# Attention scores, transpositions and products in units of 512 queries instead of 256

## The chip, the cores and the metric

The kernel runs on one core of one Trainium2 chip. The metric is the device time of one execution in microseconds (us), the median over the runs. PE is the matrix engine, DVE the vector engine, ACT the scalar engine, POOL the GpSimd engine, SP the engine that issues most loads.

## The reference

A decoder trunk of two layers on x (1024 positions, 1024 features, float32). Layer 0 is a gated linear recurrence, layer 1 is attention with a forget gate; each is followed by a SwiGLU layer, and a final norm ends it. The change touches only the attention:

```
q = (xn @ w_q) in 16 heads of 64; k, v, c come once from the residual stream
for each block of 128 queries q0:q1:
    s = q[q0:q1] @ k[:q1].T * scale + c[q0:q1, None] - c[None, :q1]
    s = where(mask, s, -inf)            # causal
    p = softmax(s)
    out[q0:q1] = p @ v[:q1]
```

## The kernel before

Every float32 product is made of three products of float32r parts (a high and a low part of each operand, `wh`/`wl`, `xh`/`xl`). Outside the attention the kernel is a stream of 128x512 matmuls. The attention runs over 8 **pairs** of heads (function `pair` of each engine, i = 0 to 7; pairs 1 to 6 are alike and are called steady here, the first and last pair have lists of their own). All engines walk through one list of steps, `pair_steps`, and each does its share of each step, in that order; semaphores tie them.

A pair has 2 heads, and a head's 1024 queries are cut into **ranges** of 256; one range of one head is a **unit**, so a pair has 8 units, in the order of `RANGE_ORDER` [3, 0, 2, 1]. The steps are:
- `A`, `B`: the value projection of this pair, 24 matmuls 128x512 each (one half of the positions), drained by DVE; `X`: eight PE transpositions of the values, copied by ACT (`X`) and DVE (`Y`).
- `S0`, `S1` in unit u: scores of the next unit's query blocks (128 queries each, width up to the diagonal) on PE; DVE subtracts the mask and takes the row maximum (L3121), ACT the exponential with the row sum (L2169). Score tiles alternate between PSUM slots 0 and 1, and a score waits until the exponential of the tile two before it has freed its slot.
- `T0`, `T1`, ...: transpositions of the probabilities (128x128 on PE, L1479) of two key blocks into `t_ps`; ACT copies them to `pth` (high part, L2204), DVE subtracts to `ptl` (low part, L3128). Both are double buffered. The first `T` of a unit waits for all exponentials of the unit.
- `V0`, `V1`, ...: products of values with `pth` and `ptl` (L1492), 256 or 128 columns wide, accumulated in `o_ps`.
- `O`: ACT copies the low half of the result (`o_low`, L2209), DVE adds it (L3137). The next unit's `V0` waits for it.
- `p`: three matmuls 128x512 of the next pair's K and Q projections, 32 `p` a pair, strewn between the others as cover (in the last pair 28 `p` of the output projection). `R`: one transposition of the row sums.

Between two pairs ACT and DVE split the next K and Q in high and low parts (L2126 to L2142 and L3047, L3053), and weight pieces are split by ACT (L1625, `HI_AT`) and DVE (L2276, `LO_AT`). POOL multiplies weights by gains (L928), scales a finished pair's output (L943) and writes the selector rows (L933).

Of the kernel before, what the change touches and what calls it, by code (L numbers as in the profile page):

```python
# [4 lines left out]
F32 = mybir.dt.float32  # L5
# [6 lines left out]
P = 128  # L12
# [37 lines left out]
class FeedForward:  # L50
# [8 lines left out]
    def first_part(self, n, half):  # L59
# [10 lines left out]
RANGE_ORDER = [3, 0, 2, 1]  # L70
UNIT_STEPS = [
# [8 lines left out]
]  # L80
FIRST_UNIT = "p p p X Y p T0 T1 p T2 V0 V1 T3 S0 S1 V2 V3"
LAST_UNIT_STEPS = [
# [8 lines left out]
]  # L91
PAIR_START = "A S0 S1 B"
FIRST_START = "A B S0 S1"
# [19 lines left out]
def pair_steps(with_p, first):  # L113

    steps = [(-1, s) for s in (FIRST_START if first else PAIR_START).split()]
    units = UNIT_STEPS if with_p else LAST_UNIT_STEPS
    for u, unit in enumerate([FIRST_UNIT] + units[1:] if first else units):
        steps += [(u, s) for s in unit.split()]
    steps.append((len(UNIT_STEPS), "O"))
    return steps  # L120


def hawk_fox_yoco(nc, x, norm_mix, norm_ffn, w_ffn_in, w_ffn_out, w_rec_in, conv_w, conv_b,
# [21 lines left out]
    RANGES = QB // 2  # L145
# [25 lines left out]
    tiles.plan("att", [1, 0, 1] + [0, 1] * (UNITS - 1) + [0], PAIRS).plan("attE", [1, 2, 0, 1, 2, 0, 1, 2, 2])  # L171
# [13 lines left out]
    T_PAIR = RANGES * (RANGES + 1)  # L185
    OUT_HI_AT = {(-1, "A"): 0, (0, "Y"): 1, (UNITS - 2, "T2"): 2}
    OUT_LO_AT = {(-1, "S1"): 0, (1, "S1"): 1, (UNITS - 2, "V2"): 2}
# [9 lines left out]
    with ExitStack() as life:  # L197
# [85 lines left out]
        with ExitStack() as att:  # L283
# [17 lines left out]
            probs = [sb(f"probs{b}", [P, 2, S // (b + 1)], F32, att) for b in range(2)]  # L301
# [4 lines left out]
            o_low = [sb(f"o_low{b}", [HD, 2 * P], F32, att) for b in range(2)]  # L306
# [48 lines left out]
        o_ps = ps[3][:, 0:2 * P]  # L355
# [369 lines left out]
        def s_tile(i, u, half):  # L725
            return tiles.use("att", half if u == 0 else 2 * u + half + 1, i)
# [6 lines left out]
        def vt_tile(i):  # L733
            return tiles.use("att", 2, i)

        def rsum_tile(i):
            return tiles.use("att", 2 * UNITS + 1, i)
# [9 lines left out]
        def tiles_before(u):  # L747

            return sum(range_of(v) + 1 for v in range(u))

        def pt_used_at(i, t):

            u = max(v for v in range(UNITS) if tiles_before(v) <= t)
            if t - tiles_before(u) == range_of(u):
                return o_filled, i * UNITS + (u + 1)
            return pt_used, i * (T_PAIR - UNITS) + (t + 1 - u)

# [148 lines left out]
        def _(pool):  # L906
# [131 lines left out]
        def _(pe):  # L1038
# [410 lines left out]
            def scores(i, u, half):  # L1449

                j, n = u // RANGES, 2 * range_of(u) + half
                acc = claim(s_tile(i, u, half))
                w = (n + 1) * P
# [9 lines left out]
            def blocks_of(r, m):  # L1463

                if m < r:
                    return [(2 * m, 0, 0), (2 * m + 1, 0, 2 * P)]
                return [(2 * m, 0, 0), (2 * m + 1, 1, 2 * P)]

            def transposes(i, u, m):
                t = tiles_before(u) + m  # L1470
                if m == 0:
                    for half in range(2):
                        slot, n = s_tile(i, u, half)
                        pe.wait_ge(drained[slot], n)
                if t >= 2 or not (isinstance(i, int) and i == 0):
                    pe.wait_ge(ptl_ready, i * T_PAIR + (t - 1))
                for kb, q0, col in blocks_of(range_of(u), m):
                    for q in range(q0, 2):
                        last = pe.transpose(t_ps[t % 2][:, col + (q - q0) * P:col + (q - q0 + 1) * P],  # L1479
                                            probs[u % 2][:, q, kb * P:(kb + 1) * P], ident[:, :])  # L1480
                last.then_inc(t_filled, 1)

            def values(i, u, m):
# [10 lines left out]
                last.then_inc(o_filled if m == r else pt_used, 1)  # L1494
# [8 lines left out]
            def pair(i, uses, with_p=True):  # L1503
# [3 lines left out]
                for u, step in pair_steps(with_p, is_first(i)):  # L1507
                    m = int(step[1]) if len(step) > 1 else 0
                    if step in "AB":
                        half = "AB".index(step)  # L1510
# [4 lines left out]
                        elif is_first(i):  # L1515
                            pe.wait_ge(f_drained, 2)
                        for k in range(KT):
                            projection_part(f_bank(step), uses["V"], half, k, v_filled)
                        f += 1
                        f_read = f_before(i) + f  # L1520
# [92 lines left out]
        def _(act):  # L1613
# [501 lines left out]
            act.activation(ps[3][0:HEADS, :], probs[0][0:HEADS, 0, :], ACT.Ln).then_inc(forget_act, 1)  # L2115
# [44 lines left out]
            def exponentials(i, u, half):  # L2160
                n, w = 2 * u + half, (2 * range_of(u) + half + 1) * P
                slot, _ = s_tile(i, u, half)
                col = u // RANGES * QB + 2 * range_of(u) + half
# [5 lines left out]
                act.activation(probs[u % 2][:, half, 0:w], ps[slot][:, score_cols(w)], ACT.Exp,  # L2169
# [11 lines left out]
            def pair(i, uses, with_p=True):  # L2181
# [4 lines left out]
                for u, step in pair_steps(with_p, is_first(i)):  # L2186
# [23 lines left out]
                    if with_p and (u, step) in HI_AT:  # L2210
                        kind = HI_AT[u, step]
# [57 lines left out]
        def _(dve):  # L2269
# [735 lines left out]
            z, e = probs[1][0:HEADS].rearrange("p a n -> p (a n)"), rinv[0:HEADS, :]  # L3005
            one_e, over = probs[0][0:HEADS, 0, :], probs[0][0:HEADS, 1, :]
# [88 lines left out]
            def pair(i, uses, with_p=True):  # L3095
# [4 lines left out]
                for u, step in pair_steps(with_p, is_first(i)):  # L3100
                    m = int(step[1]) if len(step) > 1 else 0
                    if step in "AB":
                        half = "AB".index(step)
# [3 lines left out]
                        dve.tensor_tensor(kv_tmp[:, h], f_bank(step), rstd[:, h], ALU.mult).then_inc(f_drained, 1)  # L3107
# [7 lines left out]
                    elif step[0] == "S":  # L3115
                        n, wide = 2 * (u + 1) + m, (2 * range_of(u + 1) + m + 1) * P
# [139 lines left out]
```

## Time and profile before

| | us |
|---|---|
| median of 3 runs (2226.34 to 2226.66) | 2226.61 |
| the profiled execution, its own time | 2225.23 |
| its span from first to last instruction | 2223.4 |
| PE busy | 2198.2 |
| DVE busy | 1674.6 |
| ACT busy | 1181.7 |
| one steady pair (six of them) | 60.55 |

A busy PE means that some matmul is in flight. Matmuls are pipelined, so the distance between two starts, not the duration of one, is what a matmul takes of PE's time.

### The profile page before, as it was taken

To read this page: it belongs to the slowest core of one execution; us is meant where nothing else is said; L and a number is where in the kernel's file an instruction comes from. 1 tells how busy PE (TensorE), PEld (TensorE's weight loads), DVE (VectorE), ACT (ScalarE), POOL (GpSimd) and SP (SyncE) were. 2 spreads that over 40 slices of the span, in tenths; PEclk is the share of its full clock that TensorE was granted. 3 is DMA by queue.
4 is the path that set the end of the run, shared out by engine and by line. 5 is a ranking of instruction groups with operands and counts; after the bars stand their busy time and mean duration, and the time that the engine had idled before them with its cause. 6 is when DMAs were issued, how large, how long until landed. Compare 5 with 4: busy or idle time off the path is not lost.

```text
span 2223.4 us, 28679 instructions
## 1 busy us (share of the span) xinstructions
PE 2198.2 (99%) x10393; PEld 1831.4 (82%) x10393; DVE 1674.6 (75%) x2353; ACT 1181.7 (53%) x1873; POOL 361.2 (16%) x352
## 2 busy tenths in 40 slices
PE   8999999999999999999999999999999999999998
PEld 6888887888888888887888888888888888888886
DVE  7667788787778777688666766775777778888866
ACT  5543576355555555356666666754535555555525
POOL 4000000022222222021111111102002222222200
PEclk9999999999999999999999999999999999999999
DMA  5110300366676666431111111132136666666652
GB/s 152 48 60 26 95 15 24 133 133 133 133 133 133 131 125 124 134 115 29 39 30 39 39 39 39 30 105 76 38 133 120 127 121 127 128 127 130 129 167 86
DMA packets 208984, 208.03 MB, mean 94 GB/s; under 512 B 9705, under 2 KB 153297, under 8 KB 208849
## 3 DMA queue, kind: packets, MB, share of 16 engines
q0 software_dynamic: 39168, 75.51, 20.7%
q1 hardware_dynamic: 167952, 126.43, 19.1%
q10 hardware_dynamic: 1728, 4.31, 0.7%
q8 instruction: 81, 1.33, 0.2%
q14 instruction: 55, 0.44, 0.1%
HBM read 122.28 MB, written 83.95 MB: 93 GB/s over the span
## 4 chain that ended last, share of the span: by engine, by line
PE 93%; DVE 4%; issue 1%; ACT 1%; DMA 0%; ACTq 0%; DVEq 0%
PE ps L1244 37%; PE ps L1049 18%; PE ps L1332 14%; PE ps L1445 10%; PE ps L1492 3%; PE ps L1583 3%; PE ps L1479 3%; PE ps L1460 1%; PE ps L1459 1%; PE ps L1562 1%; PE ps L1134 0%; PE ps L1525 0%; PE ps L1098 0%; PE ps L1417 0%; PE ps L1400 0%
## 5 line engine op out<-in xcount | busy, mean ns | idle before, releaser
L977 POOL DMA_DIRECT2D spill<-c x256 | 223.7, 926 | 725.5 <-DVE c L2705 493.2
L2574 DVE TENSOR_TENSOR ring_l<-raw_ffn,ring_h 128x512 fp32r<-128x512 f32 x320 | 222.8, 699 | 154.5 <-ACT ring_h L1811 153.1
L1811 ACT ACTIVATE ring_h<-raw_ffn 128x512 fp32r<-128x512 f32 x320 | 199.0, 626 | 196.5 <-PE ps L1244 103.7
L1904 ACT ACTIVATE c<-ps 128x512 f32<-128x512 f32 x256 | 150.2, 597 | 13.2
L1445 PE MATMUL ps<-xh,wh_att 128*128 128x512 f32 x368 | 148.6, 404 | 1.6 <-DVE wl_att L2276 1.6
L1811 ACT ACTIVATE ring_h<-w_sum 128x512 fp32r<-128x512 f32 x112 | 69.5, 625 | 147.2 <-PE ps L1049 38.9
L2169 ACT ACTIVATE probs<-ps,nmax 128x896 f32<-128x896 f32 (+7 forms) x128 | 95.0, 742 | 99.2 <-DVE nmax L3121 97.3
L1445 PE MATMUL ps<-xh,wl_att 128*128 128x512 f32 x368 | 143.9, 391 | 0.0
L1445 PE MATMUL ps<-xl,wh_att 128*128 128x512 f32 x368 | 143.9, 391 | 0.0
L3128 DVE TENSOR_TENSOR ptl<-ps,pth 128x512 fp32r<-128x512 f32 (+1 forms) x160 | 96.9, 634 | 52.4 <-ACT pth L2204 51.0
L2705 DVE TENSOR_TENSOR c<-ps,c 128x512 f32<-128x512 f32 x192 | 123.5, 685 | 4.8 <-PE ps L1332 4.3
L2313 DVE TENSOR_TENSOR resid<-ps,resid 128x1024 f32<-128x1024 f32 x76 | 92.4, 1221 | 39.2 <-PE ps L1049 31.4
L2204 ACT ACTIVATE pth<-ps 128x512 fp32r<-128x512 f32 (+1 forms) x160 | 82.7, 553 | 34.2 <-PE ps L1479 24.3
L1332 PE MATMUL ps<-hl,ring_h 128*128 128x512 f32 x256 | 99.8, 390 | 0.0
L1332 PE MATMUL ps<-hh,ring_h 128*128 128x512 f32 x256 | 99.7, 390 | 0.0
L1332 PE MATMUL ps<-hh,ring_l 128*128 128x512 f32 x256 | 99.6, 389 | 0.0
L3121 DVE CUSTOM_DVE_ANT_0 ps<-ps,causal 128x896 f32<-128x896 f32 (+7 forms) x128 | 94.6, 774 | 0.0
L2574 DVE TENSOR_TENSOR ring_l<-w_sum,ring_h 128x512 fp32r<-128x512 f32 x112 | 76.7, 686 | 21.9 <-ACT ring_h L1811 21.9
L1479 PE MATMUL ps<-ident,probs 128*128 128x128 f32 x576 | 81.5, 275 | 2.8 <-DVE ptl L3128 1.2
L1445 PEld LDWEIGHTS ps<-xh,wl_att 128*128 128x128 f32 x368 | 69.1, 188 | 15.6
L1492 PE MATMUL ps<-pth,vs 128*128 128x256 f32 x320 | 80.6, 279 | 0.7 <-DVE ptl L3128 0.4
L1049 PE MATMUL ps<-rxh,wh 128*128 128x512 f32 x256 | 79.9, 393 | 0.2 <-issue 0.2
(411 smaller groups left out, 6295.4 us busy)
## 6 DMA issues: line engine op xcount, KB each, us to landing
spill<-c POOLq DMA_DIRECT2D x256, 256.0 KB, 6.0
raw_ffn<-in_w_ffn_in SPq DMA_DIRECT2D x88, 512.0 KB, 5.3
raw_ffn<-in_w_ffn_out SPq DMA_DIRECT2D x44, 512.0 KB, 7.2
resid<-spill SPq DMA_DIRECT2D x24, 512.0 KB, 6.9
raw<-in_w_rec_in SPq DMA_DIRECT2D x16, 512.0 KB, 5.6
spill<-resid POOLq DMA_DIRECT2D x16, 512.0 KB, 2.9
raw_att<-in_w_kvf SPq DMA_DIRECT2D x16, 512.0 KB, 4.1
xin<-in_x SPq DMA_DIRECT2D x4, 1024.0 KB, 9.8
```

The lines of the kernel that those rows point to most:

```text
L977: pool.dma_start(spill[m, :, half * BANK:(half + 1) * BANK], block[:, :], accum_op=ALU.add).then_inc(sem, 16)
L1049: last = pe.matmul(acc[:, h], w, v[:, h], start=(first and p == 0), stop=(final and p == 2))
L1244: last = pe.matmul(acc, w, v, start=(start and k == 0 and p == 0), stop=(k == 3 and p == 2), skip_group_check=True)
L1332: last = pe.matmul(acc, a, v, start=(i in (P1, P2, P5) and p == 0), stop=(p == 2), skip_group_check=True)
L1445: last = pe.matmul(acc, w, v[:, k, h], start=(k == 0 and p == 0), stop=(k == KT - 1 and p == 2))
L1479: last = pe.transpose(t_ps[t % 2][:, col + (q - q0) * P:col + (q - q0 + 1) * P], probs[u % 2][:, q, kb * P:(kb + 1) * P], ident[:, :])
L1492: last = pe.matmul(o_ps[:, q0 * P:2 * P], v, pt[t % 2][:, col:col + n], start=(kb == 0 and pt is pth), stop=(kb == 2 * r + 1 and pt is ptl))
L1811: act.activation(F.ring_h[slot][:, :], src, ACT.Copy).then_inc(F.unit_hi, 1)
L1904: act.activation(dst[:, :], y if what == "s5" else w, ACT.Copy).then_inc(out_tapped, 1)
L2574: dve.tensor_tensor(F.ring_l[slot][:, :], src, F.ring_h[slot][:, :].bitcast(F32), ALU.subtract).then_inc(F.unit_lo, 1)
L2705: dve.tensor_tensor(c, w if what == "C22" else y, c, ALU.add).then_inc(out_joined, 1)
L3128: dve.tensor_tensor(ptl[t % 2][:, 0:width], t_ps[t % 2][:, 0:width], pth[t % 2][:, 0:width].bitcast(F32), ALU.subtract).then_inc(ptl_ready, 1)
```

## The change

A unit is now one head and 512 queries: a pair has 4 units, with `RANGE_ORDER` [1, 0] (the upper 512 queries first). A unit has four score steps `S0` to `S3`, and 3 or 7 transposed tiles of up to 512 columns. The 36 transpositions of a head stay 36, and the ten tiles of a head that ACT and DVE copy stay ten (512 wide but the last of a unit, 256, where four were 384). The product of a key block with the probabilities is up to 512 columns wide. `o_low` and its addition are 512 wide and come 4 times a pair instead of 8. `B` is cut in two (`B`, `C`, 12 matmuls each) with `S2 S3` between them, and all step lists and the tables of when weights are split are written anew; POOL scales the weights of Q ahead of the last pair's output.

```
-RANGE_ORDER = [3, 0, 2, 1]
+RANGE_ORDER = [1, 0]
 UNIT_STEPS = [
-    "T0 T1 X p p Y S0 T2 T3 p V0 V1 S1 p p V2 V3",
...
+    "T0 T1 X p S0 Y p p T2 T3 V0 S1 V1 S2 p p V2 V3 T4 T5 S3 p p p T6 V4 V5 p V6",
+    "O T0 T1 S0 S1 p V0 p T2 p S2 p S3 p V1 V2 p",
+    "S0 p O T0 T1 S1 p p V0 T2 S2 p T3 p V1 T4 V2 S3 p p V3 T5 V4 T6 p p V5 V6",
+    "T0 p O T1 p T2 p V0 V1 p R p V2 p p p",
 ]
-FIRST_UNIT = "p p p X Y p T0 T1 p T2 V0 V1 T3 S0 S1 V2 V3"
+FIRST_UNIT_STEPS = [
+    "X p Y T0 T1 p S0 p V0 T2 T3 p V1 V2 T4 S1 S2 T5 V3 V4 p T6 S3 p p V5 V6",
...
 LAST_UNIT_STEPS = [
-    "T0 T1 X Y S0 T2 p T3 V0 V1 p S1 V2 V3",
...
+    "T0 X Y T1 T2 p p V0 T3 V1 S0 V2 T4 T5 V3 S1 p p V4 T6 p S2 S3 V5 V6",
...
-PAIR_START = "A S0 S1 B"
-FIRST_START = "A B S0 S1"
+PAIR_START = "A S0 S1 B S2 S3 C"
+FIRST_START = "A B C S0 S1 p p p S2 S3 p p"
+LAST_START = "A S0 S1 B S2 S3 C"
...
             def blocks_of(r, m):
-                if m < r:
-                    return [(2 * m, 0, 0), (2 * m + 1, 0, 2 * P)]
-                return [(2 * m, 0, 0), (2 * m + 1, 1, 2 * P)]
+                if m <= 4 * r:
+                    return [(m, 0, 0)]
+                if m == 4 * r + 1:
+                    return [(m, 1, 0), (m + 2, 3, 3 * P)]
+                return [(m, 2, 0)]
...
-                    n = (2 - q0) * P
+                    n = (4 - q0) * P
                     for pt in (pth, ptl):
-                        last = pe.matmul(o_ps[:, q0 * P:2 * P], v, pt[t % 2][:, col:col + n],
-                                         start=(kb == 0 and pt is pth), stop=(kb == 2 * r + 1 and pt is ptl))
...
+                        last = pe.matmul(o_ps[:, q0 * P:BANK], v, pt[t % 2][:, col:col + n],
+                                         start=(kb == 0 and pt is pth), stop=(kb == 4 * r + 2 and pt is ptl))
...
             def pool_pair(i, uses, next_k=None):
                 pool.wait_ge(ql_ready, i * 2 + 2)
-                pool.wait_ge(o_added, i * UNITS + 1)
+                gain_piece(uses["Q"], GAIN["Q"])
                 if not (isinstance(i, int) and i == 0):
                     scale_o(i - 1)
-                gain_piece(uses["Q"], GAIN["Q"])
-                pool.wait_ge(o_added, i * UNITS + 4)
+                pool.wait_ge(o_added, i * UNITS + 2)
```

The first place is PE in a steady pair, the products of values (`vs`) with `pth` and `ptl` at the end of the pair's first unit. Before, the last two tiles (`V2`, `V3`):

```order
L1492 MATMUL ps<-pth,vs 128x256
L1492 MATMUL ps<-ptl,vs 128x256
L1492 MATMUL ps<-pth,vs 128x256
L1492 MATMUL ps<-ptl,vs 128x256
L1492 MATMUL ps<-pth,vs 128x256
L1492 MATMUL ps<-ptl,vs 128x256
L1492 MATMUL ps<-pth,vs 128x128
L1492 MATMUL ps<-ptl,vs 128x128
L1479 MATMUL ps<-ident,probs 128x128 x3
```

Now, the same place (`T6 V4 V5 p V6`):

```order
L1495 MATMUL ps<-ident,probs 128x128 x2
L1508 MATMUL ps<-pth,vs 128x512
L1508 MATMUL ps<-ptl,vs 128x512
L1508 MATMUL ps<-pth,vs 128x384
L1508 MATMUL ps<-ptl,vs 128x384
L1508 MATMUL ps<-pth,vs 128x128
L1508 MATMUL ps<-ptl,vs 128x128
L1460 MATMUL ps<-xh,wh_att 128x512
L1460 MATMUL ps<-xl,wh_att 128x512
L1460 MATMUL ps<-xh,wl_att 128x512
L1508 MATMUL ps<-pth,vs 128x256
L1508 MATMUL ps<-ptl,vs 128x256
```

Fewer and wider matmuls carry the same columns: of the 64 of 256 columns and 16 of 128 in a pair, 24 of 512, 8 of 384, 8 of 256 and 8 of 128 remain in their place.

The second place is DVE at the start of a steady pair, from the splitting of the second head's K and Q to the first low parts of probabilities (`ISA` is the mask and maximum). Before:

```order
L3047 TENSOR_TENSOR kl<-kv_tmp,kh 64x1024
L3053 TENSOR_TENSOR qs<-q_tmp,qs 64x1024
L3107 TENSOR_TENSOR kv_tmp<-ps,rstd 128x512
L3121 ISA ps,nmax<-ps,causal 128x896
L3121 ISA nmax 128x1
L3121 ISA ps,nmax<-ps,causal 128x1024
L3121 ISA nmax 128x1
L2276 TENSOR_TENSOR wl_att<-raw_att,wh_att 128x1024
L3107 TENSOR_TENSOR kv_tmp<-ps,rstd 128x512
L3128 TENSOR_TENSOR ptl<-ps,pth 128x512 x2
```

Now:

```order
L3125 TENSOR_TENSOR kv_tmp<-ps,rstd 128x512
L3139 ISA ps,nmax<-ps,causal 128x640
L3139 ISA nmax 128x1
L3139 ISA ps,nmax<-ps,causal 128x768
L3139 ISA nmax 128x1
L2294 TENSOR_TENSOR wl_att<-raw_att,wh_att 128x1024
L3139 ISA ps,nmax<-ps,causal 128x896
L3139 ISA nmax 128x1
L3139 ISA ps,nmax<-ps,causal 128x1024
L3139 ISA nmax 128x1
L3125 TENSOR_TENSOR kv_tmp<-ps,rstd 128x512
L3146 TENSOR_TENSOR ptl<-ps,pth 128x512 x2
```

Four score tiles, not two, now stand ahead of the first transposition, and the two widest come last, behind the weight split.

## Rows read from the trace of the kernel before

**Rows 1.** The page, busy time, share of the span and instructions.
```profile
PE 2198.2 (99%) x10393; PEld 1831.4 (82%) x10393; DVE 1674.6 (75%) x2353; ACT 1181.7 (53%) x1873; POOL 361.2 (16%) x352
```

**Rows 2.** Busy time by window (start:end, length), granted clock, DMA share, GB/s.
```profile
1010.00:1072.00 62.00, 58.25 (x341) 49.75 (x340) 45.99 (x80) 42.53 (x78) 7.77 (x5) 1.00 0.10 27
...
1138.55:1199.10 60.55, 60.35 (x355) 52.49 (x354) 41.40 (x77) 38.51 (x74) 10.12 (x6) 1.00 0.13 35
...
1430.00:1492.80 62.80, 61.36 (x356) 52.06 (x356) 51.47 (x87) 44.70 (x82) 0.00 (x0) 1.00 0.31 100
```

**Rows 3.** PE in order of time (start, us), one steady pair.
```profile
1142.03 1.03 PE L1479 MATMUL ps<-ident,probs 128*128 128x128 f32 x8
1143.13 1.06 PE L1525 MATMUL ps<-ident,kv_tmp 128*128 128x128 f32 x8
...
1144.27 0.39 PE L1445 MATMUL ps<-xl,wh_att 128*128 128x512 f32 x1
...
1145.60 0.95 PE L1479 MATMUL ps<-ident,probs 128*128 128x128 f32 x7
...
1146.62 0.40 PE L1445 MATMUL ps<-xl,wh_att 128*128 128x512 f32 x1
...
1148.27 0.40 PE L1445 MATMUL ps<-xh,wh_att 128*128 128x512 f32 x1
...
1149.66 0.28 PE L1492 MATMUL ps<-pth,vs 128*128 128x256 f32 x1
...
1150.37 0.22 PE L1492 MATMUL ps<-pth,vs 128*128 128x128 f32 x1
...
1150.69 0.52 PE L1479 MATMUL ps<-ident,probs 128*128 128x128 f32 x3
...
1153.26 0.22 PE L1492 MATMUL ps<-pth,vs 128*128 128x128 f32 x1
...
1153.71 0.39 PE L1445 MATMUL ps<-xl,wh_att 128*128 128x512 f32 x1
...
1154.64 0.40 PE L1445 MATMUL ps<-xh,wl_att 128*128 128x512 f32 x1
1155.17 1.07 PE L1479 MATMUL ps<-ident,probs 128*128 128x128 f32 x8
```

**Rows 4.** DVE in order of time, the same pair and the next one's start.
```profile
1152.25 0.82 DVE L3121 CUSTOM_DVE_ANT_0 ps<-ps,causal 128x640 f32<-128x640 f32 x1
...
1152.99 1.00 DVE L3121 CUSTOM_DVE_ANT_0 ps<-ps,causal 128x768 f32<-128x768 f32 x1
...
1197.05 0.69 DVE L3107 TENSOR_TENSOR kv_tmp<-ps,rstd 128x512 f32<-128x512 f32 x1
1197.66 1.09 DVE L3121 CUSTOM_DVE_ANT_0 ps<-ps,causal 128x896 f32<-128x896 f32 x1
...
1198.66 1.26 DVE L3121 CUSTOM_DVE_ANT_0 ps<-ps,causal 128x1024 f32<-128x1024 f32 x1
```

**Rows 5.** PE in order of time, first score matmul of the next pair.
```profile
1195.41 0.39 PE L1459 MATMUL ps<-kl,q 128*128 128x512 f32 x1
```

**Rows 6.** ACT in order of time, an exponential and its read of the sum.
```profile
1200.02 1.12 ACT L2169 ACTIVATE probs<-ps,nmax 128x1024 f32<-128x1024 f32 x1
1201.03 0.19 ACT L2169 ACTIVATION_READ_ACCUMULATOR probs<-ps,nmax 128x1 f32 x1
```

**Rows 7.** PE in order of time, the first pair's two longest waits.
```profile
1018.81 0.47 PE L1445 MATMUL ps<-xh,wh_att 128*128 128x512 f32 x1 [1.63 <-DVE wl_att L2276]
...
1025.11 0.66 PE L1479 MATMUL ps<-ident,probs 128*128 128x128 f32 x4 [0.83 <-DVE ptl L3128]
```

**Rows 8.** POOL in order of time.
```profile
1001.82 1.95 POOL L1022 MEMSET kl<- 64x1024 f32 x2
...
1151.93 2.40 POOL L943 TENSOR_TENSOR resid<-resid,rinv 128x1024 f32 x1 [28.94 <-DVE resid L3137]
```

**Rows 9.** Line 2276 on DVE: duration in ns, shortest, median, longest.
```profile
L2276 DVE TENSOR_TENSOR wl_att<-raw_att,wh_att x31: 1215/1220/1946, 973.4 to 1541.0; 128x1024 fp32r<-128x1024 f32 x31
```

More of the change, by code:

```diff
@@ L113, in pair_steps @@
 def pair_steps(with_p, first):
-    steps = [(-1, s) for s in (FIRST_START if first else PAIR_START).split()]
-    units = UNIT_STEPS if with_p else LAST_UNIT_STEPS
-    for u, unit in enumerate([FIRST_UNIT] + units[1:] if first else units):
+    start, units = (FIRST_START, FIRST_UNIT_STEPS) if first else (PAIR_START, UNIT_STEPS)
+    if not with_p:
+        start, units = LAST_START, LAST_UNIT_STEPS
+    steps = [(-1, s) for s in start.split()]
+    for u, unit in enumerate(units):
         steps += [(u, s) for s in unit.split()]
@@ L144, in hawk_fox_yoco @@
     QB = S // P
-    RANGES = QB // 2
+    RANGES = QB // 4
     UNITS = 2 * RANGES
@@ L184, in hawk_fox_yoco @@
     SUMMED = {seg: n * RUN_SUMS for seg, n in STAT.items()}
-    T_PAIR = RANGES * (RANGES + 1)
-    OUT_HI_AT = {(-1, "A"): 0, (0, "Y"): 1, (UNITS - 2, "T2"): 2}
-    OUT_LO_AT = {(-1, "S1"): 0, (1, "S1"): 1, (UNITS - 2, "V2"): 2}
+    T_PAIR = 2 * sum(4 * r + 3 for r in range(RANGES))
+    OUT_HI_AT = {(-1, "S1"): 0, (0, "T1"): 1, (3, "T1"): 2}
+    OUT_LO_AT = {(-1, "C"): 0, (0, "S1"): 1, (3, "V0"): 2}
     O_SPLITS = PAIRS
@@ L300, in hawk_fox_yoco @@
             vs = sb("vs", [P, 2, QB, 2, HD], F32R, att)
-            probs = [sb(f"probs{b}", [P, 2, S // (b + 1)], F32, att) for b in range(2)]
+            probs = [sb(f"probs{b}", [P, n], F32, att) for b, n in enumerate((26 * P, 10 * P))]
             pth = [sb(f"pth{b}", [P, BANK], F32R, att) for b in range(2)]
@@ L305, in hawk_fox_yoco @@
             rinv = sb("rinv", [P, S], F32, att)
-            o_low = [sb(f"o_low{b}", [HD, 2 * P], F32, att) for b in range(2)]
+            o_low = [sb(f"o_low{b}", [HD, BANK], F32, att) for b in range(2)]
             nmax = sb("nmax", [P, 2 * QB], F32, att)
@@ L723, in range_of, with s_tile, vt_tile, rsum_tile @@
             return RANGE_ORDER[u % RANGES]
-        def s_tile(i, u, half):
-            return tiles.use("att", half if u == 0 else 2 * u + half + 1, i)
+        def s_tile(i, u, n):
+            return tiles.use("att", n if u == 0 else 4 * u + n + 1, i)
+        def vt_tile(i):
+            return tiles.use("att", 4, i)
+        def rsum_tile(i):
+            return tiles.use("att", 4 * UNITS + 1, i)
+        def wide_of(u, n):
+            return (4 * range_of(u) + n + 1) * P
         def score_cols(w):
@@ L731, in score_cols, with probs_of @@
             return slice(first, first + w)
[L733 to L737, printed above, removed]
+        def probs_of(u, n):
+            first = sum(wide_of(u, q) for q in range(n))
+            return probs[u % 2][:, first:first + wide_of(u, n)]
         def f_before(i):
@@ L747, in tiles_before, with tile_wide @@
         def tiles_before(u):
-            return sum(range_of(v) + 1 for v in range(u))
+            return sum(4 * range_of(v) + 3 for v in range(u))
+        def tile_wide(u, m):
+            return BANK if m < 4 * range_of(u) + 2 else 2 * P
         def pt_used_at(i, t):
             u = max(v for v in range(UNITS) if tiles_before(v) <= t)
-            if t - tiles_before(u) == range_of(u):
+            if t - tiles_before(u) == 4 * range_of(u) + 2:
                 return o_filled, i * UNITS + (u + 1)
@@ L1447, in projection_part, with scores @@
                     last.then_inc(filled, 1)
[L1449 to L1453, printed above, removed]
+            def scores(i, u, q):
+                j, n, w = u // RANGES, 4 * range_of(u) + q, wide_of(u, q)
+                acc = claim(s_tile(i, u, q))
                 at = score_cols(w)
@@ L1471, in transposes @@
                 if m == 0:
-                    for half in range(2):
-                        slot, n = s_tile(i, u, half)
-                        pe.wait_ge(drained[slot], n)
+                    for n in range(2, 4):
+                        slot, count = s_tile(i, u, n)
+                        pe.wait_ge(drained[slot], count)
                 if t >= 2 or not (isinstance(i, int) and i == 0):
@@ L1514, in pair @@
                                 pe.wait_ge(forget_dve, INVERSE_USED)
-                        elif is_first(i):
+                        elif step == "A" and is_first(i):
                             pe.wait_ge(f_drained, 2)
[L1517 to L1520, printed above, removed]
+                        for k in {"A": range(KT), "B": range(KT // 2), "C": range(KT // 2, KT)}[step]:
+                            projection_part(f_bank("AB"[half]), uses["V"], half, k, v_filled)
+                        if step != "B":
+                            f += 1
+                            f_read = f_before(i) + f
                     elif step == "X":
```

75 lines of the change are left out of this document (40 added, 35 removed), and 20 rows, old and new, of tables (FIRST_UNIT_STEPS, LAST_UNIT_STEPS, UNIT_STEPS).

## The prediction

> **What bounds the kernel now.** I read the page first: PE is busy for 2198.2 us of the span, 99% [rows 1], so time can only come from PE's own work or from its few waits. The change touches the attention alone, some 480 us. The windows give each stretch of it: a steady pair takes 60.55 us, PE is busy 60.35 of them at the full clock (1.00, the upper of its two levels) while DVE is busy 41.40 and ACT 38.51 [rows 2]. The first pair's window has 62.00 - 58.25 = 3.75 us of idle PE, the last one's 62.80 - 61.36 = 1.44 us [rows 2]. So DVE and ACT do not bound by volume; they bound only where their chain from PE back to PE is longer than the work put between. Then PE's list in order of time, read by the distance of starts [rows 3]:
> - From 1148.27 to 1149.66 stand six 512-wide matmuls: 0.232 us each. From 1149.66 to 1150.37 six 256-wide ones: 0.118 each. Twice 0.118 is 0.237, hardly more than one 512.
> - A high/low couple of 128 columns is dear: 1153.26 to 1153.71 holds the couple and one 512, so the couple takes 0.45 - 0.23 = 0.22 us, against 0.236 for twice its columns.
> - Seven transpositions and one 512 take 1.02 (1145.60 to 1146.62), eight and one 1.14 (1143.13 to 1144.27): about 0.11 each, and some 0.03 for each change from a run of them to something else.
> - Waits of a steady pair: 1142.03 to 1143.13 is 1.10 for eight transpositions worth 0.87 (0.23, the second half of V isn't drained), 1154.64 to 1155.17 is 0.53 for one 512 (0.30, the exponentials are late), 1150.37 to 1150.69 is 0.32 for a couple of 0.22 (0.10). Together 0.63 us a pair.
>
> **PE's work after.** Columns, transpositions, scores and projections stay the same in number. In a pair 48 matmuls of 256 become 24 of 512: 48 x 0.118 = 5.66 against 24 x 0.232 = 5.57, a gain of 0.10. The other 16 of 256 and 8 couples of 128 (1.89 + 1.76 = 3.65) become 8 of 384, 8 of 256 and 4 couples of 128. No product of 384 is in the rows; by the line through 256 and 512 it is 0.175. That makes 1.40 + 0.94 + 0.88 = 3.22, a gain of 0.43. I count the runs of transpositions in the lists: 13 in a steady pair before, 16 now, 3 x 0.03 = 0.1 lost. Net 0.43 us a pair; over 8 pairs **3.5 us**. Its bounds: 0.12 us a pair if a narrow couple costs its columns alone (then only the 0.10 and 0.02 more stay), and 0.65 if the wide ones run at the best distance and the run changes cost nothing: 1.0 to 5.2 us. I take 3.5, since most of it rests on the directly read 0.22.
>
> The Trainium skill ("TensorE: Matmul & The Clock Gate", section "Back-to-back issue gap") gives the distance of warm matmuls as columns by 2.4 GHz plus 2.5 ns. By it a matmul less is worth 2.5 ns, and the 32 fewer of a pair 0.08 us, an estimate from that page of 0.6 us in all; the trace's 0.232 and the dear 128 couple disagree with it here, and the measurement decides.
>
> **The new waits of a steady pair.** The rewritten lists decide these, so I laid out by hand each place where PE comes back to DVE or ACT.
>
> *Pair start.* Today's first score begins at 1195.41 [rows 5], while DVE drains A from 1197.05 and starts its first reduction at 1197.66 [rows 4]: DVE is late by its four K and Q splits, and nothing in the change takes those away. New on PE from 1195.41: S0 0.57 (640 columns in two passes, by the distances above), S1 0.68, B 12 x 0.23, S2 0.80, ending at 1200.2, S3 until 1201.2, C until 1203.9. New on DVE from 1197.66: 0.74 and 0.91 for the two (distances in [rows 4]: 1152.25 to 1152.99, the second from its 1.00), 1.22 for the weight split [rows 9], free at 1200.5; then 1.0 for 896 columns and 1.26 + 0.1 for 1024 [rows 4], done at 1202.9. ACT's exponential and sum take 1.2 [rows 6]: 1204.1. The first transposition, due at 1203.9, waits 0.2 us. C is drained in DVE's free time right after, so the old 0.23 ahead of the values' transpositions goes. ACT also splits Q's weights here (about 1.1, with the transposed tile queued behind it); two runs of work, the eight transpositions of values and three `p` (0.7 each), cover that before V0.
>
> *Third unit.* S3 of the second unit is followed by p V1 V2 p S0 p, about 0.7 + 0.5 + 0.2 + 0.7 + 0.1 + 0.7 = 2.9 us, ahead of T0. Its reduction and exponential take 1.3 + 1.2, with DVE about 0.5 late from the tile and the reduction of S2: 3.0. Wait 0.1. V0 of the third unit comes 2 `p` after T1 and needs `o_low`, two tiles on ACT, and the low part on DVE: 2.0 to 2.2 against 1.6 plus the score: 0.1 at most.
>
> *The rest.* Every other V stands at least 1.4 us (two `p`) or another T and V behind its T. `O` is needed only at the next V0; POOL's moved work feeds splits that are due tens of us later; loads wait for the same splits and land long ahead. I price these at nothing; if the cover of one is short by half a `p`, it costs 0.3 us a pair.
>
> So 0.4 us, and I say 0.5 for what restarts cost that no layout shows, stays of 0.63: **0.8 us** gained over six pairs. Bounds: from all waits gone (-3.8) to 0.5 more than now in each pair (+3).
>
> **First and last pair.** In the first, 1.63 us went for the weight split of K and 0.83 for the low part ahead of T2 [rows 7]. The first stays (DVE's chain to it is the same, and PE comes 0.5 us earlier by narrower scores, whose other half is done later). In the new list T2 stands two `p` and more behind T0, so 0.83 goes, but V0 then waits for about 0.5 (exponential of S3, the copies of values, the low part). I take **0.6** less, bounds -2 to +1. The last pair has the same chains with DVE fuller (51.47 busy of 62.80 [rows 2]): I take no change, bounds -1 to +1.5.
>
> **Sum**, against the profiled execution: span 2223.4 - 3.5 - 0.8 - 0.6 = 2218.5. Around the span lie 2225.23 - 2223.4 = 1.8 us; the median lies 1.4 above that execution's own time. So 2226.6 - 4.9 = **2221.7 us**. From now on no difference means within 0.2%, 4.45 us: below 2222.16 is faster.
>
> **Rivals.**
> 1. *The waits eat it.* PE keeps the 0.43 us a pair, but hand layouts miss a wait of 0.5 a pair somewhere in 28 new V and T places. For it: the new pair start has no spare, and the lists were laid for one copy of each chain. Against: DVE and ACT have some 20 us a pair free. Time: 2226.6 - 3.5 + 8 x 0.5 = 2227, with half of that wait 2225.
> 2. *The narrow couple is not dear*, or the wide product brings a cost of its own (0.118 to 0.232 is already just double). Work gain 0.12 a pair, waits as forecast: 2226.6 - 1.0 - 1.4 = 2224.2.
> 3. *POOL holds DVE up: slower.* POOL's gain of Q and its scaling (2.40 us [rows 8]) now start when Q is split, on top of DVE's reductions and weight split at the pair start, where PE waits. One row speaks for it: a DVE weight split took 1946 ns instead of 1220 [rows 9] while POOL filled `kl` at 1001.82 [rows 8]. If every DVE instruction there grew by 0.6 of itself, 4 us would grow by 2.4, and T0 would wait 2.4 more in 7 pairs: +17 - 5 = 2238. It decides from 0.7 + 0.6 a pair on. Against: POOL's scaling at 1151.93 to 1154.33 ran over two reductions, which took 0.82 and 1.00 us as always [rows 4, 8].
> 4. *More than forecast*: all three steady waits gone and 0.65 of work: 2226.6 - 5.2 - 3.8 - 0.6 = 2217.
>
> The Trainium skill ("SBUF — State Buffer", section "Terms") says that DVE and GpSimd share a port pair that one of them locks for a whole instruction while the other is fully blocked. By that the scaling's 2.40 us would be paid whole in seven pairs, 17 us, an estimate of the same size as this rival's; the two reductions that ran over POOL's scaling don't show it.
>
> **How the numbers follow.** Forecast 0.48 (its own range 2219.5 to 2224), rival 1 0.23, rival 2 0.12, rival 3 0.06, rival 4 0.11. Of the forecast's cases some two thirds lie below 2222.16, of rival 4's all, of rival 1's and 2's one in five: faster 0.50. Slower is rival 3 and a tail of rival 1 over 2231: 0.08. Same 0.42. The range runs from rival 4 to the milder half of rival 1: 2216.5 to 2227.
>
> **What would show it.** Right: steady pairs of about 60.0 us; 512-wide products 0.23 apart, 384-wide 0.175; a wait of 0.2 to 0.4 at the pair's first transposition and none at the values'; PE idle of the first pair down to about 3. Wrong: a steady pair at 60.4 or more; waits named "DVE ptl" or "ACT probs" of over 0.3 us in the third unit; DVE reductions longer than 0.82 and 1.00 at the pair start while POOL is busy.

## The result, and the profile after

The changed kernel takes 2234.68 us (median of 6 runs, 2233.60 to 2235.92), the kernel before 2226.30 beside it (6 runs, 2225.53 to 2226.66). The ratio is 1.004, 95% interval 1.003 to 1.005: slower by 0.4%, where 2221.7 was forecast. The profiled execution took 2235.92 us, with a span of 2234.1.

The page of the kernel after, busy time (compare [rows 1]):

```profile
PE 2197.1 (98%) x10137; PEld 1817.7 (81%) x10137; DVE 1683.5 (75%) x2321; ACT 1177.1 (53%) x1841; POOL 360.0 (16%) x352
```

PE has 256 matmuls fewer and 1.1 us less of busy time, and yet the span grew by 10.7 us. So PE stands idle more, or is slower. DVE, with 32 instructions fewer, is busy 8.9 us longer: the first hint. The windows of the kernel after, as in [rows 2] (start:end, length; busy time of PE, of its weight loads, of DVE, ACT and POOL; granted clock, DMA share, GB/s): first pair, a steady pair, last pair, and a short piece of the first and of the last.

```profile
1010.00:1074.00 64.00, 61.26 (x317) 50.22 (x316) 46.80 (x77) 43.57 (x75) 7.73 (x5) 0.97 0.11 32
1138.10:1199.50 61.40, 59.50 (x321) 49.99 (x320) 42.94 (x73) 37.97 (x70) 10.08 (x6) 1.00 0.13 35
1435.00:1505.00 70.00, 66.18 (x341) 54.52 (x341) 53.52 (x86) 45.25 (x79) 0.00 (x0) 0.98 0.30 91
1019.00:1023.00 4.00, 3.73 (x10) 2.95 (x11) 1.83 (x5) 1.88 (x4) 0.00 (x0) 0.57 0.49 131
1472.00:1477.00 5.00, 4.07 (x13) 3.25 (x14) 4.70 (x9) 1.25 (x3) 0.00 (x0) 0.66 0.15 60
```

The steady pair of this window takes 61.40 us (61.64 on average over pairs 1 to 6), not 60.0, with 1.90 us of idle PE, where it had 0.20. And the granted clock, 1.00 in all of [rows 2], falls to its lower level in two places of the attention. The three starts that part the attention, PE in order of time (first score of pair 1, first score of the last pair, start of the projection behind the attention):

```profile
1074.95 0.30 PE L1473 MATMUL ps<-kl,q 128*128 128x320 f32 x1
...
1444.81 0.30 PE L1473 MATMUL ps<-kl,q 128*128 128x320 f32 x1
...
1502.97 0.62 PE L1600 MATMUL ps<-xh,b21h 128*128 128x512 f32 x2
```

Before, these three stand at 1074.31, 1437.61 and 1492.60. The differences, with those of two experiments below (each against the kernel before, in us of the profiled spans):

| | after | experiment 1 (late scaling) | experiment 8 (all edits) |
|---|---|---|---|
| up to pair 1 (first pair) | +0.64 | +0.50 | -1.99 |
| pairs 1 to 6 | +6.56 | -3.64 | -3.62 |
| last pair | +3.17 | +3.14 | -0.07 |
| from there to the end | +0.33 | +0.40 | -0.62 |
| span | +10.7 | +0.4 | -6.3 |

The largest waits come from the view that groups PE's waits (engine, what waited, for whom: us in total, times, longest). The line left out is the wait for the program's first load, 6.4 us after and 6.6 before:

```profile
PE ps L1495 <- ACT probs L2186: 11.1, 7, 1.9
...
PE ps L1579 <- DVE resid L3174: 2.6, 1, 2.6
PE ps L1460 <- DVE wl_att L2294: 2.1, 1, 2.1
```

**The pair start.** PE's first transposition (L1495) waits for the exponentials in each pair; the six steady pairs' waits make up 10.9 of the 11.1 us. "ACT probs" is only the last link. The chain of waits of one pair start, by start, length and what:

```profile
1202.60 0.06 DVE nmax L3139
1202.66 3.08 DVE wl_att L2294
1205.73 1.01 DVE ps L3139
...
1206.80 0.94 DVE ps L3139
...
1209.03 0.20 ACT probs L2186
...
1209.47 1.07 PE ps L1495 x8
```

The weight split stands in it with 3.08 us. The durations in DVE's list for the same place, in order of time:

```profile
1200.25 0.69 DVE L3125 TENSOR_TENSOR kv_tmp<-ps,rstd 128x512 f32<-128x512 f32 x1
1200.86 0.82 DVE L3139 CUSTOM_DVE_ANT_0 ps<-ps,causal 128x640 f32<-128x640 f32 x1
...
1201.60 1.00 DVE L3139 CUSTOM_DVE_ANT_0 ps<-ps,causal 128x768 f32<-128x768 f32 x1
...
1202.52 3.21 DVE L2294 TENSOR_TENSOR wl_att<-raw_att,wh_att 128x1024 fp32r<-128x1024 f32 x1
1205.65 1.09 DVE L3139 CUSTOM_DVE_ANT_0 ps<-ps,causal 128x896 f32<-128x896 f32 x1
```

And POOL's:

```profile
1200.41 1.90 POOL L944 TENSOR_TENSOR raw_att<-raw_att,vec 128x1024 f32<-128x1024 f32 x1 [17.48 <-DVE qs L3071]
1202.26 2.38 POOL L959 TENSOR_TENSOR resid<-resid,rinv 128x1024 f32 x1
```

POOL's scaling starts 0.26 us ahead of the split and ends at 1204.64. The split ends at 1205.73, 1.09 later: it looks as if it had waited for the scaling and then run its usual time. The drain and the two reductions, which lie over POOL's gain, keep their 0.69, 0.82 and 1.00 us. What sets them apart is their operands: each of them reads one from PSUM (`ps`), the split reads both of its own (`raw_att`, `wh_att`) from SBUF.

**The last pair.** PE, SP and DVE in order of time:

```profile
1472.93 0.50 PE L1579 MATMUL ps<-xh,wh_att 128*128 128x512 f32 x1 [2.57 <-DVE resid L3174]
```

```profile
1468.90 0.82 SPq L896 DMA_DIRECT2D resid<-spill  x2
```

```profile
1467.65 1.22 DVE L3110 TENSOR_TENSOR xl<-resid,xh 128x1024 fp32r<-128x1024 f32 x1
1472.18 0.69 DVE L3174 TENSOR_TENSOR resid<-ps,resid 128x512 f32<-128x512 f32 x1 [3.31 <-DMA resid<-spill]
```

PE needs its PSUM bank drained (L3174), the drain adds a reloaded piece of the residual, and SP sends for that piece only when DVE has made the fifth low part of the output (L3110, step `V5` of the first unit), at 1468.87. That is 24.1 us behind the first score of the last pair; before, this load was issued at 1454.58, 17.0 us behind it. Behind the wait the clock is down: the matmuls of 512 columns that start from 1473.63 to 1476.19 stand 0.42 to 0.43 us apart, not 0.23 (granted 0.66 in the window above).

**The first pair.** PE waits 2.08 us where [rows 7] has 1.63, and the matmuls behind the wait stand 0.43 apart, not 0.23:

```profile
1019.27 0.68 PE L1460 MATMUL ps<-xh,wh_att 128*128 128x512 f32 x1 [2.08 <-DVE wl_att L2294]
1019.74 0.63 PE L1460 MATMUL ps<-xl,wh_att 128*128 128x512 f32 x1
1020.17 0.63 PE L1460 MATMUL ps<-xh,wl_att 128*128 128x512 f32 x1
```

### The profile page after: what moved, and what is told of

It is laid out like the page before. It is cut to its first block, busy times and chain, and to the rows that moved or that the text cites. A ratio compares the mean times of both kernels' runs of the same rounds, so it can differ in the third digit from the quotient of the medians.

```text
span 2234.1 us, 27984 instructions
## 1 busy us (share of the span) xinstructions
PE 2197.1 (98%) x10137; PEld 1817.7 (81%) x10137; DVE 1683.5 (75%) x2321; ACT 1177.1 (53%) x1841; POOL 360.0 (16%) x352
## 4 chain that ended last, share of the span: by engine, by line
PE 88%; DVE 7%; issue 2%; ACT 2%; DMA 1%; ACTq 0%; POOL 0%; DVEq 0%; POOLq 0%
PE ps L1259 37%; PE ps L1064 18%; PE ps L1347 14%; PE ps L1460 7%; PE ps L1508 3%; PE ps L1495 3%; PE ps L1600 3%; DVE wl_att L2294 1%; DVE ps L3139 1%; PE ps L1474 1%; PE ps L1473 1%; DVE kl L3065 1%; PE ps L1579 1%; DVE qs L3071 0%; PE ps L1149 0%
## 5 line engine op out<-in xcount | busy, mean ns | idle before, releaser
L2186 ACT ACTIVATE probs<-ps,nmax 128x640 f32<-128x640 f32 (+7 forms) x128 | 94.9, 742 | 125.4 <-DVE nmax L3139 124.3
L3139 DVE CUSTOM_DVE_ANT_0 ps<-ps,causal 128x640 f32<-128x640 f32 (+7 forms) x128 | 95.6, 768 | 14.7 <-PE ps L1474 14.4
L944 POOL TENSOR_TENSOR raw_att<-raw_att,vec 128x1024 f32<-128x1024 f32 x24 | 45.3, 1898 | 371.0 <-DVE resid L3155 211.2
L1495 PE MATMUL ps<-ident,probs 128*128 128x128 f32 x576 | 83.1, 273 | 11.5 <-ACT probs L2186 11.1
L1495 PEld LDWEIGHTS ps<-ident,probs 128*128 128x128 f32 x576 | 68.7, 141 | 28.4 <-DVE kv_tmp L3125 13.2
```

The costliest lines, as they stand in the source:

```text
L3139: dve.tensor_tensor_reduce(out=ps[slot][:, score_cols(wide)], in0=ps[slot][:, score_cols(wide)], in1=causal[:, S - wide:S], scale=-1.0, sc ...
```

## The experiments

All ratios are against the kernel before, run on the same chip.

**1. The scaling put late.** POOL waits for the addition of the new pair's first unit before it scales the finished pair's output; nothing else differs from the changed kernel.

```
                 gain_piece(uses["Q"], GAIN["Q"])
                 if not (isinstance(i, int) and i == 0):
+                    pool.wait_ge(o_added, i * UNITS + 1)
                     scale_o(i - 1)
```

> The changed kernel, only POOL's scaling of a finished pair's output moved behind the second unit's result (one wait). Theory A (POOL's scaling and DVE's weight split, both between SBUF tiles, exclude each other): the weight split at a steady pair's start falls from 3.2 us to 1.22, the wait ahead of the pair's first transposition from 1.8 to some 0.2 us, a steady pair from 61.4-61.6 us to 59.8, and the time from 2234.7 to about 2224. Theory B (the chain at the pair's start is too long by its own list: four K and Q splits, four reductions, one weight split): the split's length doesn't depend on POOL, the pair stays above 61 us and the time above 2232.

Measured: 2225.32 us (10 runs, 2223.84 to 2226.09), ratio 0.9997 (0.9987 to 1.0007): 9.4 us of the loss are back by this one wait. DVE of this kernel at a pair start, and its window of a steady pair:

```profile
1198.94 1.22 DVE L2295 TENSOR_TENSOR wl_att<-raw_att,wh_att 128x1024 fp32r<-128x1024 f32 x1
1200.29 1.10 DVE L3140 CUSTOM_DVE_ANT_0 ps<-ps,causal 128x896 f32<-128x896 f32 x1
```

```profile
1137.10:1196.84 59.74, 59.60 (x321) 50.03 (x321) 41.30 (x73) 38.10 (x69) 10.14 (x7) 1.00 0.12 36
```

The split is back at 1.22. The pair from one gain of POOL to the next takes 59.74 us, and pairs 1 to 6 together 359.66, 59.94 each. The first, last and end stretches stay as in the changed kernel (table above).

**2. POOL's new order alone, in the kernel before.** Units of 256 and all old lists, but POOL's gain of Q first and the scaling right behind it, without the first wait.

```
-                pool.wait_ge(o_added, i * UNITS + 1)
+                gain_piece(uses["Q"], GAIN["Q"])
                 if not (isinstance(i, int) and i == 0):
                     scale_o(i - 1)
-                gain_piece(uses["Q"], GAIN["Q"])
```

> The kernel before with only POOL's order of the changed one: the gain of Q first, the scaling right behind it, no wait for a result. Theory A: POOL's scaling then runs from about 1199.0 to 1201.4 on the old clock, over the weight split that began at 1199.84; the split takes about 2.8 us instead of 1.22, the drain of V's second half behind it and the values' transpositions are about 1.4 us later, and a steady pair goes from 60.55 to about 62; the time to about 2235. The two reductions ahead of it keep 0.82-1.26 us. Theory B: nothing over 0.2 us a pair changes, 2226 to 2228.

Measured: 2225.91 us (10 runs, 2225.30 to 2226.35), ratio 1.000 (0.9991 to 1.001). The hold-up is there, its price isn't: I had expected about 2235. POOL and DVE of this kernel at a pair start:

```profile
1138.89 2.41 POOL L943 TENSOR_TENSOR resid<-resid,rinv 128x1024 f32 x1
```

```profile
1138.45 1.27 DVE L3120 CUSTOM_DVE_ANT_0 ps<-ps,causal 128x1024 f32<-128x1024 f32 x1
...
1139.63 2.76 DVE L2275 TENSOR_TENSOR wl_att<-raw_att,wh_att 128x1024 fp32r<-128x1024 f32 x1
1142.63 0.69 DVE L3106 TENSOR_TENSOR kv_tmp<-ps,rstd 128x512 f32<-128x512 f32 x1 [0.25 <-PE ps L1444]
```

The split again ends 1.09 behind the scaling (1142.39 against 1141.30). But in the old list both reductions that the first transposition needs stand ahead of the split, and 24 matmuls of `B` (5.4 us) are under way. The next thing on DVE, the drain, has to wait for PE, not PE for it. So the early scaling costs only together with the new list, in which the two widest reductions stand behind the split.

**3. The split put behind the reductions.** The other way round: POOL stays as in the changed kernel, and DVE splits K's weights after the reductions of `S2` and `S3`. The scaling then lies over a reduction that reads PSUM.

```
-LO_AT = {(-1, "S1"): "K", (1, "S1"): "Q", (3, "V0"): "nextV"}
+LO_AT = {(-1, "S3"): "K", (1, "S1"): "Q", (3, "V0"): "nextV"}
```

> The changed kernel with one entry of LO_AT moved: in steady pairs VectorE splits K's weights behind the reductions of S2 and S3, not ahead of them. POOL is left as it is, so its scaling now lies over these two reductions, which read and write PSUM. Theory A (only a VectorE instruction whose operands all lie in SBUF is held up until POOL's instruction has ended): the two reductions keep their 1.09 and 1.26 us, the split, started at about the scaling's end, takes 1.2 to 1.5 us, the wait of 1.80 us at the first transposition falls to about 0.3, and the time is the one of the kernel with the late scaling, about 2225.5. Theory B (POOL's scaling holds up whatever VectorE runs then): the reductions grow by about 2 us together and the first transposition still waits 1.5 us or more; about 2234. Theory C (the split costs because it stands on the chain at all, 1.22 of its 3.21 us, and POOL's share is small): half of the gain, about 2230.

Measured: 2224.87 us (11 runs, 2223.49 to 2225.51), ratio 0.9994 (0.9985 to 1.0003). Theory A stands, B and C fall. POOL and DVE of this kernel:

```profile
1198.22 2.39 POOL L959 TENSOR_TENSOR resid<-resid,rinv 128x1024 f32 x1
```

```profile
1199.83 1.10 DVE L3139 CUSTOM_DVE_ANT_0 ps<-ps,causal 128x896 f32<-128x896 f32 x1 [1.21 <-PE ps L1474]
...
1200.93 1.23 DVE L3139 CUSTOM_DVE_ANT_0 ps<-ps,causal 128x1024 f32<-128x1024 f32 x1
...
1202.08 1.22 DVE L2294 TENSOR_TENSOR wl_att<-raw_att,wh_att 128x1024 fp32r<-128x1024 f32 x1
```

The reduction of 896 columns runs 0.78 us under the scaling (1199.83 to 1200.61) and takes its 1.10. It starts when PE has written its tile, not when POOL is done. Pairs 1 to 6 take 359.61 us, the same as in experiment 1. Two edits on two engines that share only this, that split and scaling no longer meet, give the same time.

**4. The first pair's split one drain earlier.**

```
-FIRST_LO_AT = {(-1, "C"): "K", (0, "S3"): "Q", (3, "T0"): "nextV"}
+FIRST_LO_AT = {(-1, "A"): "K", (0, "S3"): "Q", (3, "T0"): "nextV"}
```

> The changed kernel, in the first pair alone the low part of K's weights is made by DVE ahead of the drain of V's second half instead of behind it. Theory A (PE's gap of 2.24 us ahead of the first p lets the granted clock fall to its lower level, which costs more than the gap itself): the gap shrinks by 0.6 us to 1.6, the clock from 1019 to 1023 stays at 1.00 as in the kernel before, whose gap was 1.8, and the time falls by 0.6 + 1.6 = 2.2 us. Theory B (the low clock has another cause, such as its place in the program): only 0.6 us come back and the clock there stays below 0.7.

Measured: 2233.88 us (5 runs, 2233.67 to 2235.70), ratio 1.004 (1.0025 to 1.0054): -0.8, not -2.2. The wait of PE only changed its name:

```profile
1018.83 0.50 PE L1460 MATMUL ps<-xh,wh_att 128*128 128x512 f32 x1 [2.00 <-DVE kv_tmp L3125]
```

The `p` behind it needs both the split and the second drain, so their order doesn't matter. The gap that theory A wanted shorter fell by 0.08 us only, so the run tests neither theory. The clock stayed at 1.00 in this profile. The three lower runs (2233.67 to 2233.88) lie where the three lower ones of the changed kernel lie (2233.60 to 2233.99); the -0.8 between the medians is a matter of how many runs lie up there (see experiment 7).

**5. The last pair's low part earlier.** The fifth low part of the output is made at `T4`, not at `V5`, of the first unit.

```
-             ... (0, "T4"): (3,), (0, "V5"): (4,),
+             ... (0, "T4"): (3, 4),
```

> The changed kernel, in the last pair alone the fifth low part of O is made at T4 with the fourth and not at V5. Theory A (the reload of the residual from DRAM, 3.2 us, starts only behind that low part, DVE's first sum of the output projection waits for it and with DVE everything behind): the load is issued 3 us earlier, the 3.3 us of idle DVE and the 2.7 us gap of PE near 1470 go, the clock there stays 1.00, and the time falls by 2.7 + some 1.5 for the clock, less up to 1 us for tiles that the low part now holds up: about 3 us. Theory B (the last pair is bound by DVE's volume): the gap moves elsewhere, less than 1 us.

Measured: 2232.48 us (8 runs, 2230.64 to 2233.70), ratio 1.0029 (1.0018 to 1.004). The load goes out at 1465.07, 3.8 us earlier; the wait of 2.57 is gone, and the clock does not fall there. A smaller wait came up:

```profile
1466.70 0.50 PE L1473 MATMUL ps<-kl,q 128*128 128x512 f32 x1 [0.76 <-ACT probs L2186]
```

The last pair takes 54.83 us in this profile, against 58.16 in the changed kernel and 54.99 before. The medians show 2.2 of these 3.3 us; this is left open.

**6. The row sums' step earlier, on top of experiment 1.** `R` of the last unit stands behind `T1`. Behind `R` hangs a chain at the very end (reciprocal, store, load, scaling, splitting), for which PE waited 0.80 us at 1513.46 in the changed kernel.

```
-    "p O T0 T1 p p T2 V0 R V1 p p p V2 p",
+    "p O T0 T1 R p p T2 V0 V1 p p p V2 p",
```

> The changed kernel with POOL's scaling later and R behind T1. Theory A (the store of the reciprocal row sums is issued late, behind DVE's last weight split, and its load, POOL's scaling, the high and the low part of O wait for it in a row): the store is issued some 2.5 us earlier, the load is then bound by the last unit's result alone, about 0.5 us earlier, and the wait of 0.8 us ahead of the last rows of the output projection falls to 0.3 or less: 2224.7. Theory B (the chain is bound by the last unit's result anyway): the wait stays at 0.8 us and the time at 2225.3.

Measured: 2223.19 us (10 runs, 2222.65 to 2225.27), ratio 0.9991 (0.9982 to 1.000). In its profile no such wait is left, and the stretch behind the attention is 1.1 us shorter than in experiment 1. The other 1.0 of the 2.1 us between the two medians is most likely the clock's, not the edit's: the mean granted clock of a run is 0.997 in nine of the ten runs of experiment 1, and in four of the ten here, the four slowest. The clock stayed up in the first pair, although PE had waited as long as in the changed kernel:

```profile
1018.79 0.47 PE L1461 MATMUL ps<-xh,wh_att 128*128 128x512 f32 x1 [2.08 <-DVE wl_att L2295]
1019.09 0.39 PE L1461 MATMUL ps<-xl,wh_att 128*128 128x512 f32 x1
1019.32 0.40 PE L1461 MATMUL ps<-xh,wl_att 128*128 128x512 f32 x1
```

From the end of this wait to pair 1 it is 54.08 us here, and 55.68 in the changed kernel: the lower clock costs 1.6 us.

**7. Mends together.** Experiments 1, 4, 5 and 6 in one kernel, and the same without 4.

> The four edits together on the changed kernel: POOL's scaling later, the first pair's split of K ahead of the second drain, the fifth low part of O at T4, and in the last unit of the last pair the transposition of the row sums (R) behind T1 instead of behind V0. Theory A (the losses lie apart: POOL's hold on DVE, the clock after the first gap, the reload, the tail) has them add up: 2234.7 - 10 - 1.5 - 2.5 - 0.9 = 2219.8, so that the units of 512 queries are 6 us faster than the kernel before, as the sum of the prediction had it without its slower rival (2221.7). Theory B (one chain is behind several of them) has them overlap: 2223 to 2225, no difference from the kernel before.

Measured: 2220.57 us (11 runs, 2219.01 to 2222.09), ratio 0.9975 (0.9966 to 0.9984).

> The same without the first pair's edit: POOL's scaling later, the fifth low part of O at T4, R behind T1. Beside the run of all four edits it prices the first gap and its clock where nothing else waits. Theory A: the clock after the first gap is at its lower level in most executions and costs 1.5 to 2 us: 2221.5. Theory B (the clock falls only now and then): the same time as with all four, within 0.5 us.

Measured: 2221.07 us (11 runs, 2219.06 to 2222.00), ratio 0.9977 (0.9968 to 0.9987). Experiment 4's edit is worth 0.5 us at most, less than the runs scatter. The times of both kernels lie in two groups (up to 2219.6 and from 2220.5 on, with nothing between), as those of the changed kernel do (three of 2233.6 to 2234.0, three of 2235.4 to 2235.9). The groups are two clocks: each run of the upper group has a mean granted clock of 0.998 and each of the lower one of 0.999 in these two kernels, 0.997 and 0.998 in the changed one. The two profiles here are of the upper group, and in both the clock is down behind the first pair's wait.

**8. The wait itself made shorter.** As 1, 5 and 6 together; and in the first pair DVE drains the second half of the projection first, then splits, then drains the first half.

```
-                        half = "AC".index(step)
+                        half = ("CA" if is_first(i) else "AC").index(step)
...
-FIRST_LO_AT = {(-1, "C"): "K", (0, "S3"): "Q", (3, "T0"): "nextV"}
+FIRST_LO_AT = {(-1, "A"): "K", (0, "S3"): "Q", (3, "T0"): "nextV"}
```

PE's wait ahead of its first `p` asks for one drain fewer.

> This is the kernel with all three mends (late scaling, low part of the residual given out earlier in the last pair, rinv's step behind the first transposition of the last unit), and in the first pair VectorE now drains the second half of the projection first, then splits K's weights, then drains the first half, so that the first transposition hangs on two short operations fewer behind the split. Theory A (the clock falls because TensorE stands idle over about 2 us there): the gap ahead of the first transposition falls from 2.0 to 2.1 to about 1.5 us, the granted clock of 1019 to 1023 stays 1.00 in the profile and the runs no longer fall into two clumps 1.7 us apart; about 2219. Theory B (the fall of the clock does not hang on that gap's length): the clumps stay, and the time is about 2220 to 2221.

Measured: 2219.07 us (7 runs, 2218.81 to 2219.49), ratio 0.9971 (0.9960 to 0.9982), the fastest of all, 6.6 us under the kernel before. The wait is shorter, the clock stays up and the second group of times is gone (a mean granted clock of 0.999 in all seven runs). The runs lie where experiment 7's lower groups lie (2219.01 to 2219.59), so what the edit brings is the clock, hardly the 0.5 us of wait:

```profile
1017.97 0.47 PE L1461 MATMUL ps<-xh,wh_att 128*128 128x512 f32 x1 [1.48 <-DVE wl_att L2295]
1018.28 0.40 PE L1461 MATMUL ps<-xl,wh_att 128*128 128x512 f32 x1
```

## Why the prediction was wrong, and where it was right

**Right: PE's work.** The 0.43 us a pair was taken from distances of narrow products. Products after, in the kernel of experiment 1:

```profile
1157.30 0.34 PE L1509 MATMUL ps<-pth,vs 128*128 128x384 f32 x1
1157.48 0.35 PE L1509 MATMUL ps<-ptl,vs 128*128 128x384 f32 x1
1157.66 0.22 PE L1509 MATMUL ps<-pth,vs 128*128 128x128 f32 x1
...
1158.12 0.39 PE L1461 MATMUL ps<-xl,wh_att 128*128 128x512 f32 x1
```

384 columns take 0.18 (forecast 0.175), a couple of 128 and a 512 take 0.46 together (0.45 in [rows 3]). Where split and scaling don't meet, a steady pair takes 59.94 us; 0.43 + 0.13 less than 60.55 is 59.99. So the terms "3.5" and "0.8" of the sum hold together over the six steady pairs (3.4 us forecast, 3.6 and 3.7 in experiments 1 and 3), and with POOL's hold taken away rivals 1 and 2 fall. The work's share in the first and the last pair wasn't measured apart. The change of unit size is a gain, by 3.6 us over the six steady pairs.

Of the formula that it quotes for the distance of matmuls the prediction left out a condition. The Trainium skill ("TensorE: Matmul & The Clock Gate", section "Back-to-back issue gap") gives it for an isolated matmul, and says itself that at few columns it counts too little, as it leaves the weight loads out. Here each matmul has a weight load (10393 of both in [rows 1]), so the couple of 128, 0.22 us in [rows 3], doesn't speak against that section. The forecast's sum didn't use the formula.

**Wrong: the pair start.** The step that failed is the layout "*Pair start*", which takes "1.22 for the weight split" and has DVE free at 1200.5. It kept POOL out, though the change moves POOL's scaling to this very place; the text put that into rival 3, with a chance of 0.06, and priced POOL's moved work "at nothing". Rival 3 was the mechanism, but not in its form: not every instruction grows by 0.6 of itself, only the split waits, and it waits to the scaling's end (3.21 us, not 1.22). Put into the same layout, that gives a scaling from 1.90 us behind Q's splitting to 1201.4, a split until 1202.4, 1.9 later than forecast, and over six steady pairs (in the last pair DVE scales, not POOL) 2221.7 + 11.4 = 2233. Measured are 10.2 us over these pairs, 369.86 against 359.66. Rival 3 had reckoned with seven pairs, where POOL scales in six; and the sign named for it, longer reductions at the pair start, could not have shown it, as these kept their 0.82 and 1.00.

**Two rows were misread.** The argument against rival 3, that the scaling "ran over two reductions, which took 0.82 and 1.00 us as always", is true and says nothing of the split, as these read PSUM. And the 1.95 us of [rows 9] were put down to POOL's filling of `kl` [rows 8]. POOL ahead of that fill, and DVE beside it, in the kernel before:

```profile
999.16 2.59 POOL L933 CAST q<-negsel 64x1024 fp32r<-64x1024 f32 x2
```

```profile
1000.88 1.95 DVE L2276 TENSOR_TENSOR wl_att<-raw_att,wh_att 128x1024 fp32r<-128x1024 f32 x1
1002.75 1.21 DVE L3069 SCALAR_TENSOR_TENSOR probs<-probs,rinv 16x1024 f32<-16x1024 f32 x1
```

The casts end at 1001.75 and the split at 1002.83, 1.08 later: the same figure as in both kernels above. [rows 9] show the longest split alone; the same line has one of 1.88 us, beside a POOL multiplication between SBUF tiles:

```profile
1517.64 2.41 POOL L964 TENSOR_TENSOR sq_att<-sq_att 128x1024 f32<-128x1024 f32 x1 [1.18 <-ACT sq_att L1652]
```

```profile
1519.25 1.88 DVE L2276 TENSOR_TENSOR wl_att<-raw_att,wh_att 128x1024 fp32r<-128x1024 f32 x1 [2.23 <-ACT wh_att L1625]
```

It ends at 1521.13, again 1.08 behind POOL's 1520.05. A third one, of layer 0, took 3.42 us (from 37.63) under such a multiplication. The fill, which reads nothing, lay over the rest of the split and over the next instruction, which also has two SBUF operands, and cost neither anything. The whole rule was in the trace of before, had the end of the long instruction been set beside the ends on POOL and not only its length beside the others.

The Trainium skill ("SBUF — State Buffer", section "Who interferes with whom") says just this: a DVE instruction with two SBUF inputs contends with a GpSimd instruction that reads SBUF, not with one that only writes it, and a DVE instruction with at most one SBUF input, outside DVE's 2-port modes, doesn't contend. The traces agree in all three: 3.21 and 2.76 us over the scaling, 1.21 over a fill, 0.82, 1.00 and 1.10 over gains and scalings. The prediction had weighed the shorter rule of the section "Terms" of the same page of the Trainium skill and let the reductions speak against it.

**Wrong in size: the last pair.** "I take no change, bounds -1 to +1.5"; it was +3.17. The term was carried over from the other pairs, without following what the moved low part of the output releases, a DMA. Experiment 5 takes that wait away, and with it 3.3 us in its profile and 2.2 in the medians.

**The first pair.** "The first stays" was 1.63 and became 2.08: PE comes 0.5 us earlier, as the text itself said, so it waits longer for a DVE chain that hasn't moved. With the clock up (experiment 6) the forecast is met and more: from the pair's first score to pair 1 it is 57.69 us (1015.18 to 1072.87) against 59.11 before (1015.20 to 1074.31), 1.4 less, where 0.43 of work and the 0.6 make 1.0. The 0.5 us that it expected ahead of V0 doesn't show: behind 1019 PE's only listed wait in this pair is 0.2. The lower clock took 1.6 back in three of the changed kernel's six executions.

## What to carry to other kernels

When POOL's work is moved, look at what stands on DVE in the same microseconds, by operands: here one with both inputs in SBUF waited until a reading POOL instruction that was already running had ended, and one that reads PSUM didn't. Whether it costs is decided by what stands behind the held instruction; order the list so that nothing which the bound engine waits for does. And where a step is moved in the last, fullest stretch, follow each DMA that it releases.

## What the runs showed of the hardware

- A split of 128x1024 (1.22 us alone), started under a reading POOL instruction, ended 1.08 to 1.09 us behind that instruction's end, in the kernel before (1.95 and 1.88 us long), the changed one (3.21) and experiment 2 (2.76); POOL's scaling took its 2.38 to 2.41 us all the same.
- TensorE's clock fell to the lower of its two levels behind the last pair's wait of 2.54 to 2.75 us in all five profiles that have it (granted 0.66 or 0.67 over 5 us in the changed kernel and experiments 1, 3, 4 and 6). Behind the first pair's wait of 2.00 to 2.09 us it fell in six profiles (0.57 to 0.65 over 4 us: the changed kernel, experiments 1, 3, 5 and both of 7) and not in two (experiments 4 and 6). Behind waits of 1.48 to 1.63 us (before, experiments 2 and 8) it didn't. What decides it between equal waits is not settled.
